# One wide matmul for the high and the low half of the activations, in the first product of the second block's feed-forward

## The reference, cut to what matters

```python
x = x + jnp.einsum('bse,ed->bsd', y, w_out[l])
h = rms_norm(x, norm_mlp[l])
u = jnp.square(jax.nn.relu(jnp.einsum('bsd,df->bsf', h, w_ff1[l])))
x = x + jnp.einsum('bsf,fd->bsd', u, w_ff2[l])
return rms_norm(x, norm_final)
```

## Time and profile before

| | |
|---|---|
| median of 3 runs | 729.62 us (728.57 to 731.13) |
| the profiled execution | 729.17 us, of which the profile's span is 727.4 us |
| TensorE busy | 703.8 us, 97% of the span |
| VectorE busy | 536.6 us, 74% |
| ScalarE busy | 389.9 us, 54% |
| mean granted TensorE clock | 0.997 |
| the last stage (ff1 and ff2) | from about 541 us to the end |

### The profile page before, as it was taken

The page is one execution under the profiler, slowest core; times in us unless marked ns, Lnnn a source line. Parts: engine busy times, 40 slices in busy tenths (PEclk is TensorE's granted clock), DMA queues, the critical chain, the costliest instruction groups (busy, mean ns, idle before and its releaser), DMA issues.

```text
span 727.4 us, 14604 instructions
## 1 busy us (share of the span) xinstructions
PE 703.8 (97%) x6156; PEld 663.6 (91%) x6156; DVE 536.6 (74%) x953; ACT 389.9 (54%) x599; POOL 24.0 (3%) x50
## 2 busy tenths in 40 slices
PE   6989999999999999999999999999999999999997
PEld 6988998888999999999999999888899998998995
DVE  6899798556988877777768798965976655666653
ACT  7477368356366354444445683488664334434443
POOL 3010000000000000000000240000000000000000
PEclk9999999999999999999999999999999999999999
DMA  8741153223555555555555544333345655565541
GB/s 248 220 157 60 59 174 118 62 95 139 172 173 177 174 178 194 200 183 174 179 193 196 188 128 164 122 100 125 125 148 181 204 191 176 196 209 174 182 166 58
DMA packets 94700, 115.66 MB, mean 159 GB/s; under 512 B 7971, under 2 KB 83932, under 8 KB 94636
## 3 DMA queue, kind: packets, MB, share of 16 engines
q1 hardware_dynamic: 94244, 114.51, 48.1%
q0 software_dynamic: 128, 0.13, 0.1%
q10 hardware_dynamic: 264, 0.10, 0.1%
HBM read 113.69 MB, written 1.05 MB: 158 GB/s over the span
## 4 chain that ended last, share of the span: by engine, by line
PE 75%; DVE 14%; ACT 7%; issue 3%; POOL 0%; DVEq 0%; ACTq 0%; POOLq 0%
PE psum L1821 16%; PE psum L1822 15%; PE psum L1823 15%; DVE w_lo L1084 4%; PE psum L2397 4%; PE psum L2395 4%; PE psum L2396 4%; ACT w_hi L501 3%; PE psum L2162 2%; PE psum L2164 2%; PE psum L2160 2%; PE psum L1968 1%; PE psum L2003 1%; PE psum L1913 1%; PE psum L2218 1%
## 5 line engine op out<-in xcount | busy, mean ns | idle before, releaser
L1084 DVE TENSOR_TENSOR w_lo<-w_raw,w_hi 128x2048 fp32r<-128x2048 f32 x105 | 239.3, 2287 | 70.9 <-ACT w_hi L501 70.8
L501 ACT ACTIVATE w_hi<-w_raw 128x2048 fp32r<-128x2048 f32 x105 | 199.0, 1906 | 54.6 <-PE psum L2397 36.6
L1821 PE MATMUL psum<-x2n_hi,w_hi 128*128 128x256 f32 x400 | 114.4, 286 | 2.7 <-DVE x2n_lo L1541 1.3
L1822 PE MATMUL psum<-x2n_lo,w_hi 128*128 128x256 f32 x400 | 111.9, 280 | 0.0
L1823 PE MATMUL psum<-x2n_hi,w_lo 128*128 128x256 f32 x400 | 111.9, 280 | 0.0
L1821 PE MATMUL psum<-hs_hi,w_hi 128*128 128x256 f32 (+1 forms) x352 | 99.5, 283 | 0.0
L1822 PE MATMUL psum<-hs_lo,w_hi 128*128 128x256 f32 (+1 forms) x352 | 99.1, 281 | 0.0
L1823 PE MATMUL psum<-hs_hi,w_lo 128*128 128x256 f32 (+1 forms) x352 | 98.9, 281 | 0.0
L1821 PEld LDWEIGHTS psum<-x2n_hi,w_hi 128*128 128x128 f32 x400 | 75.2, 188 | 6.3 <-DVE x2n_lo L1541 2.3
L1823 PEld LDWEIGHTS psum<-x2n_hi,w_lo 128*128 128x128 f32 x400 | 76.2, 191 | 0.0
L1822 PEld LDWEIGHTS psum<-x2n_lo,w_hi 128*128 128x128 f32 x400 | 75.1, 188 | 0.6
(11 more groups left out here) (459 smaller groups left out, 1530.2 us busy)
## 6 DMA issues: line engine op xcount, KB each, us to landing
w_raw<-in_w_ff_dram SPq DMA_DIRECT2D x32, 1024.0 KB, 5.3
w_raw<-in_w_in_dram SPq DMA_DIRECT2D x27, 1024.0 KB, 5.3
w_raw<-in_w_up_dram SPq DMA_DIRECT2D x22, 1024.0 KB, 5.1
w_raw<-in_w_down_dram SPq DMA_DIRECT2D x11, 1024.0 KB, 5.0
w_raw<-in_w_o_dram SPq DMA_DIRECT2D x4, 1024.0 KB, 5.1
w_raw<-in_w_out_dram SPq DMA_DIRECT2D x4, 1024.0 KB, 5.4
w_raw<-in_w_ssm_out_dram SPq DMA_DIRECT2D x2, 1024.0 KB, 5.1
w_raw<-in_w_att_out_dram SPq DMA_DIRECT2D x2, 1024.0 KB, 5.0
```

Of the source, the lines that this page charges most:

```text
L501: A.activation(w_hi[:, u % NW, :], raw[:, u % NRAW, :], ACT.Copy).then_inc(sem("hi_ready"), 1)
L1084: V.tensor_tensor(w_lo[:, u % NRAW, :], raw[:, u % NRAW, :], w_hi[:, u % NW, :].bitcast(F32), ALU.subtract).then_inc(sem("lo_ready"), 1)
L1821: T.matmul(out_, lh, rh, start=start, stop=False)
L1822: T.matmul(out_, lh, rl, start=False, stop=False)
```

## The change

The two halves of the normed activations come to lie in one tile, `x2n_two`, so that one access takes 256 columns of the high half and 256 of the low half. A new TensorE function `ff1` takes the place of `unit` in the last stage: for each kt one matmul of 512 columns (w_hi with both halves) and one of 256 (w_lo with the high half, added into columns 0 to 255). The bank then holds high x high + low x high in columns 0 to 255 and high x low in columns 256 to 511. ScalarE copies columns 256 to 511 into `uu`, VectorE adds columns 0 to 255 to them, and a further VectorE instruction does maximum and factor. ScalarE's `split_to` is now called behind the copy of group m = 0. Besides, the four transfers into `lamv` signal `par_in` as well, and all who wait for `par_in` now wait for 25 transfers.

```diff
-        x2n_hi = sb("x2n_hi", [P, KD, 256], F32R, k(64))
-        x2n_lo = sb("x2n_lo", [P, KD, 256], F32R, k(8768))
+        x2n_two = sb("x2n_two", [P, 2, KD * 256 + 64], F32R, k(64))
+        x2n_hi, x2n_lo = (x2n_two[:, i, 0:KD * 256].rearrange("p (k t) -> p k t", k=KD) for i in range(2))
...
-                        par(sp, "lam_in", lamv[:, i], ins[key].to_broadcast([P, 64]))
+                        par(sp, "par_in", lamv[:, i], ins[key].to_broadcast([P, 64]))
...
             for i in range(KF2 // 2):
-                split_to(unit_at[("ff1", i)]["n"] + 3)
                 for m in range(2):
-                    taken(act, group(("ff1", i), m))
+                    g = group(("ff1", i), m)
+                    act.wait_ge(sem("group_done"), g + 1)
+                    need(act, "u_lo", 2 * (i - 2) + m + 1)
+                    A.activation(uu[:, i % 2, m, :], banks[g % NB][:, 256:512], ACT.Copy).then_inc(sem("halves"), 1)
+                    if m == 0:
+                        split_to(unit_at[("ff1", i)]["n"] + 3)
+                for m in range(2):
+                    act.wait_ge(sem("relu"), 2 * i + m + 1)
                     if i >= 2:
                         used(act, unit_at[("ff2", i - 2)]["n"])
                     A.activation(u_hi[:, i % 2, m, :], relu[:, i % 2, m, :], ACT.Square).then_inc(sem("u_hi"), 1)
...
-            dve.wait_ge(sem("lam_in"), 64)
+            dve.wait_ge(sem("par_in"), 16 * 25)
...
                     r = relu[:, i % 2, m, :]
-                    STT(out=r, in0=banks[g % NB][:, 0:256], scalar=0.0, in1=rst2[:, :], op0=ALU.max,
-                        op1=ALU.mult).then_inc(sem(f"group_free{g % NB}"), 1)
+                    dve.wait_ge(sem("halves"), 2 * i + m + 1)
+                    tt(r, uu[:, i % 2, m, :], banks[g % NB][:, 0:256], ALU.add).then_inc(
+                        sem(f"group_free{g % NB}"), 1)
+                    taken(dve, g)
+                    STT(out=r, in0=r, scalar=0.0, in1=rst2[:, :], op0=ALU.max, op1=ALU.mult).then_inc(sem("relu"), 1)
...
+            def ff1(i, between=None):
+
+                u = unit_at[("ff1", i)]
+                un = u["n"]
+                pe.wait_ge(sem("lo_ready"), un + 1)
...
+                for m in range(2):
+                    g = u["g0"] + m
+                    need(pe, f"group_free{g % NB}", free_count(g))
+                    c = slice(P * m, P * m + P)
+                    for kt in range(KD):
...
+                        T.matmul(banks[g % NB][:, :].rearrange("p (a t) -> p a t", a=2), wh[:, kt, c],
+                                 x2n_two[:, :, 256 * kt:256 * kt + 256], start=kt == 0, stop=False,
+                                 skip_group_check=True)
+                        last = T.matmul(banks[g % NB][:, 0:256], wl[:, kt, c], x2n_hi[:, kt, :], start=False,
+                                        stop=kt == KD - 1, skip_group_check=True)
+                    last.then_inc(sem("group_done"), 1)
...
-            param_cols(2, "par_in", 21)
-            param_cols(3, "par_in", 21)
+            param_cols(2, "par_in", 25)
+            param_cols(3, "par_in", 25)
...
             for i in range(KF2 // 2):
-                unit("ff1", i, x2n, 8, ready=None if i else "x3_lo",
-                     between=(x3_stat, x3_turn)[i] if i < 2 else None)
+                ff1(i, between=(x3_stat, x3_turn)[i] if i < 2 else None)
                 if i:
                     ff2(i - 1)
```

More of the change, by code:

```diff
@@ L1789, in _ @@
                     r = relu[:, i % 2, m, :]
-                    STT(out=r, in0=banks[g % NB][:, 0:256], scalar=0.0, in1=rst2[:, :], op0=ALU.max,
-                        op1=ALU.mult).then_inc(sem(f"group_free{g % NB}"), 1)
+                    dve.wait_ge(sem("halves"), 2 * i + m + 1)
[3 more added lines that the diff above has]
+                    STT(out=r, in0=r, scalar=0.0, in1=rst2[:, :], op0=ALU.max, op1=ALU.mult).then_inc(sem("relu"), 1)
                 for m in range(2):
-                    taken(dve, group(("ff1", i), m))
+                    dve.wait_ge(sem("relu"), 2 * i + m + 1)
                     r = relu[:, i % 2, m, :]
@@ L1854, in unit @@
                             last = mm3(bank[:, 0:256], ah[:, kt, c], al[:, kt, c], wh[:, kt, :], wl[:, kt, :], a, z)
+                    last.then_inc(sem("group_done"), 1)
+                    if between and m == 0:
+                        between()
+            def ff1(i, between=None):
+                u = unit_at[("ff1", i)]
+                un = u["n"]
+                pe.wait_ge(sem("lo_ready"), un + 1)
+                wh = w_hi[:, un % NW, :].rearrange("p (k n) -> p k n", k=KD)
+                wl = w_lo[:, un % NRAW, :].rearrange("p (k n) -> p k n", k=KD)
+                for m in range(2):
[3 more added lines that the diff above has]
+                    for kt in range(KD):
+                        if i == 0 and m == 0:
+                            pe.wait_ge(sem("x3_lo"), kt + 1)
+                        T.matmul(banks[g % NB][:, :].rearrange("p (a t) -> p a t", a=2), wh[:, kt, c],
[3 more added lines that the diff above has]
+                                        stop=kt == KD - 1, skip_group_check=True)
                     last.then_inc(sem("group_done"), 1)
```

## The result

| | before | after |
|---|---|---|
| median of 4 runs, us | 729.66 (728.57 to 731.13) | 767.12 (762.39 to 767.31) |
| ratio, 95% interval | | 1.0495 [1.0467, 1.0524] |
| profiled execution, us | 729.17 | 767.04 |
| its span, us | 727.4 | 765.1 |
| mean granted clock of its span | 0.997 | 0.986 |

What follows compares the result with a forecast made beforehand. TensorE, busy 97% of the span, was taken as the bound. Fourteen ff2 late by 1.97 us (27.6) less 0.3 us gain gave +27.3 on 729.17 us; stated 756.7 us, own range 753.5 to 760.5, widened to 752.5 to 766.

Steps and rivals of the forecast that it cites:

- What bounds it: Whole kernel: TensorE, busy for 97% of the span, so its idle time costs in full; it never waits in the last stage.
- the delay of the split: Last stage: ff2's weight split waits for half of ff1 i, making ff2 1 to 14 each 1.97 us late, 27.6 us.
- The seven terms: Last stage: times from ff1 i's first matmul to ff2's start, 7.62 us in place of 5.65.
- Steps 1 to 7: Last stage, in order: first group, ScalarE's start, PSUM copy, w_hi, VectorE's start, w_lo, TensorE's start; ending at 7.62 us.
- Step 1, the first group: ff1's first 8 wide and 8 narrow matmuls: last narrow one starts at 2.64 us and ends at 2.92.
- The bound for such errors: Seven terms, each good to 0.05 us or so: claimed at most 0.2 us for each of 14 beats, 2.8 us.
- TensorE's gain: ff1: joining two 256-column matmuls into one of 512 saves 0.0087 us, at most 2.2 us over 256 pairs.
- the clock falls in the stalls: TensorE's idle time before ff2 drops its clock to 1.2 GHz, 1.6 us a fall; 779 or 768 us; chance 9%.
- the split is not held up: Last stage: w_hi copy ready for TensorE by 5.5 us, so only the gain remains, 727.4 us; chance 5%.
- the two-piece matmul is slow: ff1's wide matmul costs twice as much, 0.45 us, beat 14.87 us, about 789 us; chance 4%.
- What is late next: Last stage: second w_lo ends at 9.66 us, wanted at 13.06; added VectorE work is covered, ff2 15 having 0.4 us to spare.
- the layout and the signal: The tile joining the halves and the renamed signal for transfers into lamv: claimed to cost nothing.

Runs made afterwards that it cites:

- Run 2: Kernel before, with ScalarE waiting for the first group of ff1 i ahead of its splits, nothing else changed: 755.21 us, ratio 1.0338.
- Run 5: Changed kernel with the split call back at the iteration's head and activation halves side by side, so wide matmuls read 512 adjacent columns: 730.20 us, ratio 1.0013.
- run 4: Changed kernel with the split call back at the iteration's head and each wide matmul again two of 256 columns: 730.38 us, ratio 1.0007.
- run 9: Changed kernel with the split call back at the iteration's head and each group's eight wide matmuls ahead of its eight narrow ones: 728.32 us, ratio 1.000.
- run 1: Changed kernel with only ScalarE's split call moved back to the head of each iteration: 729.84 us, ratio 0.9999.
- Runs 2 and 7: Run 2 has its own line; 7 is the changed kernel plus one useless 512-column matmul ahead of the wait of ff2 1 to 14: 758.96 us.
- Run 8: Kernel before, with the joint tile for the two halves and the lamv transfers signalling par_in: 728.14 us, ratio 0.9993.
- run 6: Kernel before, with ScalarE's wait for the first ff1 group plus one useless PSUM copy ahead of the splits: 763.86 us, ratio 1.049.

## Why the prediction was right, and where it was wrong

- **What bounds it, and the delay of the split: right.** The seven terms add up to 7.62 us and 1.97 us a beat; the trace shows 2.06. Single terms: copy to split 0.29 us (606.16, then 606.45) against 0.27; `w_hi` to `w_lo` 1.94 (606.45, then 608.39) against 1.93; the copy itself 0.38. Idle time 1.78 us, 14 times, against 1.8. Run 2 gives the delay without the copy. Steps 1 to 7 hold for ff2 1 to 14 and for no other.
- **Step 1, the first group: short by 0.07 us.** It is 8 x 0.235 + 7 x 0.118 = 2.71 us, not 2.64. This and some hundredths make 2.06 of 1.97, 1.3 us in all. (The bound for such errors was added up wrongly: seven terms of 0.05 us make 0.35 us a beat, 4.9 us in all, not 0.2 and 2.8. The error that came, 0.09, is inside either.)
- **"TensorE's gain", taken from the pace of L2395: wrong.** I read the difference between ff1's 0.1177 us for 256 columns and ff2's 0.2267 for 512 as a cost of each matmul, which joining would save once: 0.0087 us a pair. Run 5 has an ff1 matmul of the same width from one piece, and it takes 0.235; run 4 shows nothing lost by parting it. The difference is one of pace per column, 0.459 ns in ff1 and 0.443 in ff2; in ff1 it is the same for both widths, but for the reordered narrow matmuls of run 9. The upper bound that I had written beside it, 0.2354 us, is what came. The 2.5 ns a matmul that the Trainium skill states (TensorE: Matmul & The Clock Gate, Back-to-back issue gap) were nearer than my 9 ns, but the traces don't show them either: by them a unit of 16 pairs would be 0.04 us shorter, and it is 0.004 us shorter (run 1 against run 4).
- **The rival "the clock falls in the stalls": given 9%, and it came.** This is the step that put the median outside the range, some 8 of the 10.4 us. Its price was right: 1.6 us a fall was estimated from the early fall, and 1.6 was measured. Its frequency was not: I had worked out every beat, 779 us, and every other, 768; it came behind five stalls of 14. The other 2.4 us are the 1.3 us of the longer beats, the 0.3 us of gain that ff1 0 and ff1 1 didn't have, and the 0.7 us ahead of the first ff2. The range had been widened to 766 us for falls in some beats, which is room for five of them and for little else. What failed was the reason against it: that TensorE had kept its clock from 46 to 50 us, busy for only 1.81 of 4 us. That row shows one stretch, once, and tells nothing of one gap of 1.8 us in each of 14 beats. TensorE's timeline of the kernel before shows what it is made of, two gaps of 1.45 and 1.05 us:

```profile
47.73 0.66 PE L1943 MATMUL psum<-ident,bb 128*128 128x128 f32 x4 [1.45 <-ACT b_blk L587]
48.22 1.04 PE L1943 MATMUL psum<-ident,b_blk 128*128 128x128 f32 x8
50.30 0.92 PE L1943 MATMUL psum<-ident,b_blk 128*128 128x128 f32 x6 [1.05 <-ACT BT L594]
```

Both are shorter than the 1.50 us that brought no fall in run 2. From about 16 us to its last matmul, the kernel before has no gap of TensorE as long as 1.5 us, so nothing in its trace said that the clock would survive 1.8 us. Runs 2 and 7 show how near the edge the case was: at 1.50 and 1.55 us idle the clock fell behind none of 28 stalls.

- **The rival "the split is not held up": wrong, as said.** `w_hi` starts 3.3 us into ff1.
- **The rival "the two-piece matmul is slow": wrong as priced.** It costs what two narrow ones cost.
- **"What is late next", the layout and the signal: right.** The second `w_lo` ends at 612.88, and no matmul waits for it; the added adds and copies cost nothing beside the wait (run 1 has them all, and loses nothing). Run 8 has the layout and the signal. The busy time of VectorE and ScalarE grew by 11.2 and 9.1 us, less than the 13 and 12 foretold; for ScalarE the reason is in the rows, since the next instruction starts 0.29 us after a copy of 0.38 us, and 32 x 0.29 is about 9.

What stays open: which of the stalls of 1.78 us bring a fall. After the change it was every third or fourth, five of 14; in run 6 three of 14, the first of them the 5th; the stalls themselves are alike, and no run was made to tell them apart. Also open is why ff1 and ff2 have different paces.

No version beats the kernel before: runs 1, 4, 5 and 9 can't be told from it (their intervals reach from 0.9981 to 1.0033). Who wants the wide matmul should keep the splits ahead of the wait; there is then nothing lost, and nothing gained.

## What to carry to other kernels

Before adding a wait to an engine that works its list in order, look at what stands behind it: here a copy that nobody was in a hurry for held up the split that TensorE needed next, and the one wait alone costs 25 us in the kernel before. Evidence that a gap is harmless has to be a gap of that length: a mean over a longer stretch can hide that it is made of shorter ones. A short idle gap of TensorE can cost more than its length, because the clock may fall behind it; when such gaps recur, price the fall into the range, and try whether a useless matmul in the gap, or a gap some tenths shorter, takes it away. Before counting on a gain from joining matmuls, compare the pace per column within the same loop, not with a neighbouring one.

## What the hardware showed beyond that

- Falls of the clock depended on a few tenths of a microsecond: 28 stalls of 1.50 and 1.55 us had none, 28 of 1.78 us had eight, each of some 3.4 us at 1.2 GHz and 1.6 us of lost time. The eight falls began 0.2 to 0.6 us after TensorE had gone on. One useless matmul per beat took the change's five away, and its median is 8.2 us below the change's.
- Matmuls of this type have two paces at a granted clock of 1.00: 0.113 to 0.114 or 0.118 us for 256 columns, 0.227 or 0.233 to 0.235 for 512. They go with the place in the program (in the kernel before, the medians of 20 us stretches are 0.114 from 420 to 460 us, 0.118 from 460 to 500, and 0.118 in the last stage), and in run 9 with the order, not with the number of pieces.
